# Half of the key page products of a paged decode moved from VectorE to GpSimd, in a hybrid decoder layer

## The chip, the core and the metric

One core of one Trainium2 chip runs the whole kernel in one launch. The metric is the device time of that core in microseconds. Engines are TensorE (PE), VectorE (DVE), ScalarE (ACT), GpSimd (POOL) and SyncE (SP); POOL and SP also issue the kernel's DMAs.

## What is computed

One inference step of one decoder layer, for a prompt of 256 tokens and for 8 samples of one token each (264 columns together). Width 2048; a combined input projection feeds two groups of heads: 8 heads of stick-breaking attention (head size 128) and 4 heads of gated linear attention; then an output projection and a SwiGLU FFN. The samples attend to a paged cache: 8 samples x 8 pages = 64 key pages and 64 value pages, each 128 positions x 8 heads x 128. The part that the change touches is the score of the samples against the cached keys:

```python
k_past = cache_k[l][page_table].reshape(dec_b, -1, SB_HEADS, SB_HEAD_DIM)
...
k_all = jnp.concatenate([k_past.astype(h.dtype), k_rows], axis=1).transpose(0, 2, 1, 3)
...
z = jnp.einsum('bhqd,bhkd->bhqk', q.astype(jnp.float32), k.astype(jnp.float32)) * (SB_HEAD_DIM ** -0.5)
...
a = jnp.where(mask, jnp.exp(log_beta + tail), 0.0)
return jnp.einsum('bhqk,bhkd->bhqd', a, v.astype(jnp.float32))
```

For one page and one sample this is, for each of 128 positions (partitions) and each head, the sum over 128 elements of key times query.

## The kernel before, in words

**Weight units and slots.** The input projection and the output projection are cut into 128 units of two 128-row blocks by 512 columns (groups of 8 units). Each unit goes through a ring of four buffers: SP loads it (`w_load`, L398), ACT makes a rounded high part (`hi`, L723, L727), DVE the low part (`lo`, L1275, L1277), and PE multiplies high and low parts with high and low parts of the activations, three products each (`products`, L1996 to L1999; `unit`, L2001). The program of each engine is a loop over slots, `st` in `range(NSLOT)`: in slot `st` PE multiplies unit `st`, ACT and DVE begin with the parts of unit `st + 3`, and behind that every engine does what is written by hand for this slot. ACT's high part waits until PE has used the unit four earlier, SP's load until the low part of the unit four earlier is made. Conditioning weights come as `ada_r` tiles of 1 MB in SP's queue (`ada_load`, L401), and PE uses one of them at the end of many slots (L1931).

**The decode path.** `KP_SLOT` says in which slot key page `n` is worked on: three pages in two slots from slot 20 to 31, one page a slot from 32 to 49, three in two slots from 50 to 68. PE spreads the query of a sample over all partitions (`query_rows`, L2025), ACT copies it to `QBC` (`q_bcast`, L802, L808; two buffers). Then:
- DVE, in slot `KP_SLOT[n]` behind its low part: `page_product` (L1316). An even page takes eight multiplications of 128x128 that also sum the head (L1328, semaphore `k_even`). An odd page takes one multiplication of 128x1024 in place (L1322, semaphore `k_mul`).
- ACT, in the slot after, near its end: `page_sums` (L810, L815) waits for `k_mul` and sums the eight heads of an odd page (semaphore `k_odd`). At the end of every eighth slot the evacuations of a group (`evac`, L729) stand behind it.
- POOL: `k_page` (L564 to L577) reads the page number from the table, waits until the page five earlier is done (`k_even` or `k_odd`, L572), and requests the page; five pages are in flight or in work. The request for page `n` stands in slot `KP_SLOT[n - 5] + (n - 5) % 2`: so a request that needs an odd page's sums stands in the slot in which ACT makes them, a request that needs an even page in the slot in which DVE multiplies it.

**Behind it.** In slots 47 and 70 DVE takes the scores of four samples each, in slots 53 and 76 ACT makes the weights, and PE multiplies them with value pages, two a slot (`page_values`, L2115, L2129), in slots 56, 57 and from 60 on (`AV_SLOT`). POOL requests value pages (`v_page`, L579, L595) in the same slots, each after PE has used the page five earlier. POOL also stores the states (`state_store`, L603) and rows of keys.

**The tree of the linear attention.** In slots 31 to 50, beside the key pages: DVE takes differences (`tree_diff`, L1335) in odd slots, ACT their exponential (`tree_exp`, L818) and DVE the products (`tree_product`, L1355) in even slots, PE multiplies (`tree_mm`, L2041, L2055) in odd slots, from slot 33 on.

The order of POOL's queue in one slot is: key page requests, value page requests, state store, stores of key rows:

```python
for n in range(5, TS * PAGES):
    if s == KP_SLOT[n - 5] + (n - 5) % 2:
        k_page(n)
...
if s in AV_AT:
    for m in (2 * AV_AT[s] + 5, 2 * AV_AT[s] + 6):
        if m < TS * PAGES:
            v_page(m)
if s in DEC_AT and DEC_AT[s] % 3 == 2:
    state_store(DEC_AT[s] // 3)
```

Of the kernel before, what the change touches and what calls it, by code (L numbers as in the profile page):

```python
# [10 lines left out]
ALU = mybir.AluOpType  # L11
# [7 lines left out]
def stickbreak_gla_layer(nc, x_prompt, x_sample, c_prompt, c_sample, cache_k, cache_v, page_table, state_gla,  # L19
# [10 lines left out]
    H = b_sb.shape[1]  # L30
    DH = g_sb_out.shape[1]
# [3 lines left out]
    PAGES = page_table.shape[1]  # L35
# [17 lines left out]
    with ctx:  # L53
        def sem(name):
            return ctx.enter_context(nc.semaphore(name))

        def sems(name, n):
            return [sem(f"{name}{i}") for i in range(n)]
# [7 lines left out]
        def put(name, shape, dt=F32, at=None):  # L66
            size = 4
            for s in shape[1:]:
                size *= s
            size = -(-size // 32) * 32  # L70
            if at is None:
                at = cursor[0]
                cursor[0] += size
            assert at + size <= top, (name, at + size, top)
            return nc.alloc_sbuf_tensor_at(name, shape, dt, offset=at)
# [81 lines left out]
        KPG = [put(f"k_page{i}", [P, HS], at=a) for i, a in enumerate(  # L157
            (r0 + 38016, r0 + 42112, r0 + 46208, r0 + 50304, r0 + 62592, r0 + 21120, r0 + 92544))]
# [7 lines left out]
        QBC = put("q_bcast", [P, 2, HS], at=r0 + 66688)  # L166
# [8 lines left out]
        ZD = put("z_dec", [P, TS, PAGES * H], at=r0 + 74880)  # L175
# [105 lines left out]
        KP_AT = {s: [n for n in range(TS * PAGES) if KP_SLOT[n] == s] for s in KP_SLOT}  # L281
        KP_PLACE = [n % 5 if n % 5 < 4 else 4 if n < 34 else 5 if n < 54 else 6 for n in range(TS * PAGES)]
# [34 lines left out]
        kpage_in = sems("kpage_in", 5)  # L317
# [17 lines left out]
        srow_ready, qlo_ready, qb_mm, qb_ready = sem("srow_ready"), sem("qlo_ready"), sem("qb_mm"), sem("qb_ready")  # L335
        k_mul, k_even, k_odd = sem("k_mul"), sem("k_even"), sem("k_odd")
# [190 lines left out]
        def _(pool):  # L527
            link = linker(pool, pool_own)
            g = nc.gpsimd
# [34 lines left out]
            def k_page(n):  # L564
                page = pool.value_load(PT[0:1, n:n + 1], min_val=0, max_val=NPOOL - 1)
                if n == 2:
                    pool.wait_ge(ada_used, 14)
                if n == 34:

                    pool.wait_ge(alp_ready, 1)  # L570
                if n >= 5:
                    pool.wait_ge(k_odd if (n - 5) % 2 else k_even, (n - 5) // 2 + 1)  # L572
                if n == 54:

                    pool.wait_ge(g_o, GH)
                pool.dma_start(KPG[KP_PLACE[n]][:, :], pool_k[bass.ds(page, 1), :, :].rearrange("o p n -> p (o n)"))\
                    .then_inc(kpage_in[n % 5], 16)  # L577

            def v_page(m):  # L579
                if m in (0, 1):  # L580
                    pool.wait_ge(kft_tr, 1)
                elif m == 2:
                    pool.wait_ge(g_st, 1)
                elif m == 3:
                    pool.wait_ge(vg_tr, 4)
                    pool.wait_ge(vsmp_ready, 1)
                elif m == 4:
                    pool.wait_ge(g_o, GH)
                else:
                    pool.wait_ge(av_used, (m - 5) // 2 + 1)  # L590
                if m == 32:
                    pool.wait_ge(k_even, 32)
                    pool.wait_ge(k_odd, 32)
                page = pool.value_load(PT[0:1, m:m + 1], min_val=0, max_val=NPOOL - 1)
                pool.dma_start((VPA if m < 32 else VPB)[m % 5][:, :],  # L595
                               pool_v[bass.ds(page, 1), :, :].rearrange("o p n -> p (o n)")).then_inc(vpage_in[m % 5], 16)

            def zero_rows():

                pool.wait_ge(ada_used, 32)  # L600
                g.memset(VGS[:, :].bitcast(F32), 0.0).then_inc(pool_made, 1)

            def state_store(c):  # L603
                h, half = divmod(c, 2)
                pool.wait_ge(dec_taken, 3 * c + 2)
                pool.dma_start(new_state_sample[0, 4 * half:4 * half + 4, h].rearrange("b k v -> k b v"),
                               SS[:, c % 3, :, :]).then_inc(state_out[c % 3], 16)
# [5 lines left out]
            for s in range(20, 97):  # L613
                if s == 58:

                    v_page(4)
# [3 lines that stand above are left out]
                if s in (53, 55):  # L620
                    v_page(s - 53)
                    v_page(s - 52)
                if s == 56:
                    pool.wait_ge(gla_copied, 2)
                    pool.dma_start(new_state_prompt[0, 0].rearrange("h k v -> k h v"), SFIN[:, :, :]).then_inc(sfin_out, 16)
                if s == 58:
                    zero_rows()
# [3 lines that stand above are left out]
                            v_page(m)  # L631
                if s in DEC_AT and DEC_AT[s] % 3 == 2:
                    state_store(DEC_AT[s] // 3)
                if s - 2 in KT_AT:
                    i = KT_AT[s - 2]
                    grp, tb = divmod(i, 2)
                    pool.wait_ge(kt_ready, i + 1)
                    pool.dma_start(kv_rows[tb * P:(tb + 1) * P, grp * 512:grp * 512 + 512], KTOK[i % 2][:, :])\
                        .then_inc(ktok_out[i % 2], 16)
# [24 lines left out]
            for m in range(MT - 1):  # L664
                pool.wait_ge(gm_ready, NOUT + 2 * m + 1)
                ins = g.tensor_tensor(SQD[:, 8, :], SQD[:, 8, :], SQD[:, X_LAST[m], :], ALU.add)
# [523 lines left out]
        def _(dve):  # L1190
            link = linker(dve, dve_own)
            v = nc.vector
# [123 lines left out]
            def page_product(n):  # L1316
                b = n // PAGES
                kp = KPG[KP_PLACE[n]]
                dve.wait_ge(kpage_in[n % 5], 16 * (n // 5 + 1))
                dve.wait_ge(qb_ready, 2 * b + 2)  # L1320
                if n % 2:
                    v.tensor_tensor(kp[:, :], kp[:, :], QBC[:, b % 2, :], ALU.mult).then_inc(k_mul, 1)  # L1322
                else:

                    pg = n % PAGES
                    for h in range(H):
                        hs = slice(h * DH, (h + 1) * DH)
                        ins = v.scalar_tensor_tensor(kp[:, hs], kp[:, hs], 1.0, QBC[:, b % 2, hs], ALU.mult, ALU.mult,  # L1328
                                                     accum_out=ZD[:, b, pg * H + h:pg * H + h + 1])
                    ins.then_inc(k_even, 1)  # L1330

            def halves(t, n):
                return t.rearrange("p h (j n) -> p h j n", n=n)
# [172 lines left out]
            def slot(st):  # L1506
# [38 lines left out]
                if st == 61:  # L1545
                    dve.wait_ge(srow_ready, 3)
                    for j in range(2):
                        cs = slice(j * 512, j * 512 + 512)
                        ins = v.tensor_tensor(VGS[32:32 + TS, cs], ps[0:TS, 5 + j, :], VGS[0:TS, cs].bitcast(F32),
                                              ALU.subtract)  # L1550
                    ins.then_inc(qlo_ready, 1)
                if st == 17:
                    dve.wait_ge(srow_ready, 1)
                    for half in range(2):
                        cs = slice(half * 512, half * 512 + 512)
                        ins = v.tensor_tensor(QHL[32:32 + TS, cs], ps[0:TS, 6 + half, :], QHL[0:TS, cs].bitcast(F32),
                                              ALU.subtract)
                    ins.then_inc(qlo_ready, 1)
                for n in KP_AT.get(st, ()):
                    page_product(n)  # L1560
                if st == 25:
                    dve.wait_ge(bank_out, 12)
                    v.tensor_scalar(PGQ[:, 0:GH, :], PGQ[:, 0:GH, :], GLA_SCALE, None, ALU.mult).then_inc(alp_ready, 1)
# [37 lines left out]
                if st == 87:  # L1601
                    dve.wait_ge(row_tr, 4)
                    for vb in range(VD):
                        ins = v.tensor_copy(PGQ[:, vb::VD, TP:T].rearrange("p h (f j) -> p h f j", f=2),
                                            ps[:, 4, vb * P:(vb + 1) * P].rearrange("p (j c) -> p j c", j=4)[:, :, 0:2 * GH]
                                            .rearrange("p j (h f) -> p h f j", f=2))
# [9 lines left out]
                if st == 89:  # L1616
                    dve.wait_ge(silu_r, 8)
                    dve.wait_ge(norm_sq, 1)
                    for vb in range(VD):
                        cs = slice(vb, 8, VD)  # L1620
                        ins = v.scalar_tensor_tensor(PGQ[:, cs, :], PGQ[:, cs, :], vec2[:, V2["gla"] + vb:V2["gla"] + vb + 1],
                                                     PR[:, cs, :], ALU.mult, ALU.mult)
# [98 lines left out]
            for st in range(NSLOT):  # L1721
                slot(st)
# [130 lines left out]
            for j in range(1, 5):  # L1853
                for u in range(4):
                    lo_n(j * 4 + W_DOWN, u)
                    k = 4 * j - 4 + u
                    ins = v.transpose(XT[:, :, k, :], X[:, k, 0:TP].rearrange("p (b j) -> p b j", j=32))  # L1857
# [33 lines left out]
            for m in range(8):  # L1891
                dve.wait_ge(tail_sq, m + 1)
                ins = v.tensor_tensor(F_LO[:, 0, :], F_LO[:, 0, :], F_LO[:, 8 + m, :], ALU.add)
# [674 lines left out]
```

## Time and profile before

| What | Value |
|---|---|
| Median of 3 runs | 1488.83 us (1487.38 to 1489.83) |
| Profiled execution, its own time | 1489.45 us |
| Its span, first to last instruction | 1487.7 us |
| Busy PE / DVE / ACT / POOL | 1428.6 / 922.3 / 665.3 / 105.8 us |
| Mean granted clock of PE | 0.983 of full speed |
| Moved by DMA | 396.82 MB, mean 267 GB/s |

The time lies 1.75 us above the span; what is worked out on the span is taken to move the time by as much. PE is busy for 96% of the span, but matmuls are pipelined and their ends are modelled, so busy PE is not PE at its peak; what matters is where it is idle. Busy shares are averages over stages: slots 20 to 68, in which key pages are worked on, take about 188 to 420 us of the span; the FFN takes the second half.

### The profile page before, as it was taken

Reading aid. Unit: us, or ns where it says so; the run is one execution under the profiler, and the core shown is the slowest. Engines: PE = TensorE matmul, PEld = TensorE weight load, DVE = VectorE, ACT = ScalarE, POOL = GpSimd, SP = SyncE. Lnnn points to the kernel's source line nnn. Section 1 sums busy time; section 2 is a strip of 40 time slices with the busy share of each in tenths; the row PEclk is TensorE's granted clock in tenths of the full one; section 3 lists DMA queues with packets and bytes.
Section 4 is the critical chain, followed back from the end, with each engine's and each line's share of the span. In section 5 each row is a group of like instructions: output and inputs, shape, how many; then the busy total and the mean of one; then the engine's idle time right before and its main releaser. Section 6 shows DMA issues by size and latency. Waiting matters only on the chain.

```text
span 1487.7 us, 29187 instructions
## 1 busy us (share of the span) xinstructions
PE 1428.6 (96%) x11232; PEld 1270.8 (85%) x11232; DVE 922.3 (62%) x1519; ACT 665.3 (45%) x1303; POOL 105.8 (7%) x203
## 2 busy tenths in 40 slices
PE   7779999999899999999999999999999999999997
PEld 2237787887668787796999999999999999999997
DVE  2234588996778667369856766566665675446444
ACT  1023477677655554445543434334344343334333
POOL 0000311113322210000000000000000000200000
PEclk9969999999899999999999999999999999999999
DMA  9999999999999979987666666665666655855552
GB/s 368 421 341 359 388 392 406 379 345 397 392 396 336 342 258 354 404 323 278 221 181 184 178 179 179 181 185 171 183 181 174 185 173 190 233 179 181 182 177 95
DMA packets 139330, 396.82 MB, mean 267 GB/s; under 512 B 13162, under 2 KB 17681, under 8 KB 126433
## 3 DMA queue, kind: packets, MB, share of 16 engines
q1 hardware_dynamic: 117954, 319.59, 63.1%
q0 software_dynamic: 21232, 76.10, 13.5%
q8 instruction: 49, 0.80, 0.2%
q14 instruction: 31, 0.25, 0.0%
q10 hardware_dynamic: 64, 0.07, 0.0%
HBM read 382.28 MB, written 11.34 MB: 265 GB/s over the span
## 4 chain that ended last, share of the span: by engine, by line
PE 84%; DMA 9%; DVE 3%; ACT 2%; issue 1%; POOLq 0%; SPq 0%; POOL 0%; DVEq 0%; ACTq 0%
PE ps L1997 24%; PE ps L1998 24%; PE ps L1999 24%; PE ps L1931 4%; DMA ada_s<-in_w_ada 4%; DMA v_page<-in_cache_v 2%; PE ps L2129 2%; DMA ada_r<-in_w_ada 1%; DMA k_page<-in_cache_k 1%; PE ps L2055 1%; ACT k_page L815 1%; PE ps L1974 0%; DVE k_page L1328 0%; DVE w_lo L1277 0%; ACT w_hi L727 0%
## 5 line engine op out<-in xcount | busy, mean ns | idle before, releaser
L1997 PE MATMUL ps<-h_hi,w_hi 128*128 128x264 f32 x2304 | 666.9, 289 | 6.1 <-DVE h_lo L1265 3.6
L1998 PE MATMUL ps<-h_lo,w_hi 128*128 128x264 f32 x2304 | 658.6, 286 | 0.0
L1999 PE MATMUL ps<-h_hi,w_lo 128*128 128x264 f32 x2304 | 658.2, 286 | 0.0
L1997 PEld LDWEIGHTS ps<-h_hi,w_hi 128*128 128x128 f32 x2304 | 438.1, 190 | 49.1 <-issue 33.6
L1822 DVE TENSOR_TENSOR w_lo<-raw,w_hi 128x1024 fp32r<-128x1024 f32 x254 | 307.2, 1214 | 273.1 <-ACT w_hi L1059 271.7
L1059 ACT ACTIVATE w_hi<-raw 128x1024 fp32r<-128x1024 f32 x264 | 278.5, 1059 | 403.2 <-PE ps L1999 391.0
L1998 PEld LDWEIGHTS ps<-h_lo,w_hi 128*128 128x128 f32 x2304 | 437.4, 190 | 0.5
L1999 PEld LDWEIGHTS ps<-h_hi,w_lo 128*128 128x128 f32 x2304 | 436.3, 189 | 0.0
L1277 DVE TENSOR_TENSOR w_lo<-raw,w_hi 128x1024 fp32r<-128x1024 f32 x138 | 168.8, 1224 | 144.4 <-ACT w_hi L727 143.9
L727 ACT ACTIVATE w_hi<-raw 128x1024 fp32r<-128x1024 f32 x128 | 135.1, 1056 | 174.7 <-PE ps L1999 156.3
L1998 PE MATMUL ps<-act_lo,w_hi 128*128 (+1 forms) x704 | 200.5, 285 | 0.0
L1997 PE MATMUL ps<-act_hi,w_hi 128*128 (+1 forms) x704 | 200.2, 284 | 0.0
L1999 PE MATMUL ps<-act_hi,w_lo 128*128 (+1 forms) x704 | 199.7, 284 | 0.0
L1997 PEld LDWEIGHTS ps<-act_hi,w_hi 128*128 128x128 f32 x704 | 132.5, 188 | 0.3 <-issue 0.2
L1998 PEld LDWEIGHTS ps<-act_lo,w_hi 128*128 128x128 f32 x704 | 132.6, 188 | 0.0
L1999 PEld LDWEIGHTS ps<-act_hi,w_lo 128*128 128x128 f32 x704 | 132.5, 188 | 0.0
L1815 DVE RECIPROCAL glu<-glu 128x264 f32<-128x264 f32 x44 | 78.8, 1792 | 0.0
L815 ACT ACTIVATE k_page<-k_page 128x128 f32<-128x128 f32 x256 | 75.2, 297 | 7.0 <-DVE k_page L1322 6.8
L1931 PE MATMUL ps<-ada_r,c_t_keep 128*32 128x512 f32 x512 | 66.3, 603 | 4.2 <-DMA ada_r<-in_w_ada 4.2
L1328 DVE SCALAR_TENSOR_TENSOR k_page<-k_page,q_bcast 128x128 f32<-128x128 f32 x256 | 56.9, 289 | 11.5 <-DMA k_page<-in_cache_k 11.4
L1931 PE MATMUL ps<-ada_s,c_t_keep 128*32 128x512 f32 x256 | 45.9, 799 | 18.1 <-DMA ada_s<-in_w_ada 18.1
L675 POOL DMA_DIRECT2D x_moved_blocks<-x_blocks x16 | 8.6, 546 | 585.2 <-DVE x_blocks L1857 585.2
(363 smaller groups left out, 1217.6 us busy)
## 6 DMA issues: line engine op xcount, KB each, us to landing
ada_r<-in_w_ada SPq DMA_DIRECT2D x64, 1024.0 KB, 8.9
raw<-in_w_in SPq DMA_DIRECT2D x96, 512.0 KB, 8.4
raw<-in_w_ffn_gate SPq DMA_DIRECT2D x88, 512.0 KB, 3.7
raw<-in_w_ffn_up SPq DMA_DIRECT2D x88, 512.0 KB, 3.8
raw<-in_w_ffn_down SPq DMA_DIRECT2D x88, 512.0 KB, 4.3
ada_s<-in_w_ada SPq DMA_DIRECT2D x32, 1024.0 KB, 13.2
k_page<-in_cache_k POOLq DMA_DIRECT2D x64, 512.0 KB, 7.9
v_page<-in_cache_v POOLq DMA_DIRECT2D x38, 512.0 KB, 8.0
```

The costliest lines, as they stand in the source:

```text
L727: s.activation(HI[:, u % 4, :], RAW[:, u % 4, :], ACT.Copy).then_inc(hi_ready, 1)
L815: ins = s.activation(kp, kp, ACT.Copy, accum_out=ZD[:, b, pg * H + h:pg * H + h + 1])
L1059: s.activation(HI[:, u % 4, :], RAW[:, u % 4, :], ACT.Copy).then_inc(hi_ready, 1)
L1277: v.tensor_tensor(LO[:, u % 4, :], RAW[:, u % 4, :], HI[:, u % 4, :].bitcast(F32), ALU.subtract)\
L1328: ins = v.scalar_tensor_tensor(kp[:, hs], kp[:, hs], 1.0, QBC[:, b % 2, hs], ALU.mult, ALU.mult, accum_out=ZD[:, b, pg * H + h:pg * H + h ...
L1815: v.reciprocal(GLU[:, m, :], GLU[:, m, :]).then_inc(glu_step, 1)
L1822: v.tensor_tensor(LO[:, u % 4, :], RAW[:, u % 4, :], HI[:, u % 4, :].bitcast(F32), ALU.subtract)\
L1931: ins = mm(ps[32 * j:32 * j + 32, bank, :], CTK[:, k, :], ring[:, j * CG:(j + 1) * CG], start=(k == 0), stop=(k == KC - 1))
L1997: mm(out, w_hi, xh, start=first, stop=False)
L1998: mm(out, w_hi, xl, start=False, stop=False)
L1999: return mm(out, w_lo, xh, start=False, stop=last)
L2129: ins = mm(ps[32 * j:32 * j + 32, 7, :], AD[:, b % 4, 2 * pair + j // 2, :], page, start=(v % 16 == 0), stop=(v % 16 == 15))
```

## The change

The product of an odd key page is no longer made by DVE in slot `KP_SLOT[n]` but by POOL in the same slot, behind POOL's key page requests, value page requests and state store of that slot. POOL waits there for the landing of the page and for the spread query. DVE keeps the even pages. ACT's sums, the requests and all slots stay as they are.

```diff
+            def odd_product(n):
+                kp = KPG[KP_PLACE[n]]
+                pool.wait_ge(kpage_in[n % 5], 16 * (n // 5 + 1))
+                pool.wait_ge(qb_ready, 2 * (n // PAGES) + 2)
+                g.tensor_tensor(kp[:, :], kp[:, :], QBC[:, n // PAGES % 2, :], ALU.mult).then_inc(k_mul, 1)
+
             def v_page(m):
...
                 if s in DEC_AT and DEC_AT[s] % 3 == 2:
                     state_store(DEC_AT[s] // 3)
+                for n in KP_AT.get(s, ()):
+                    if n % 2:
+                        odd_product(n)
                 if s - 2 in KT_AT:
...
                 dve.wait_ge(qb_ready, 2 * b + 2)
-                if n % 2:
-                    v.tensor_tensor(kp[:, :], kp[:, :], QBC[:, b % 2, :], ALU.mult).then_inc(k_mul, 1)
-                else:
-
-                    pg = n % PAGES
-                    for h in range(H):
...
+                pg = n % PAGES
+                for h in range(H):
...
                 for n in KP_AT.get(st, ()):
-                    page_product(n)
+                    if n % 2 == 0:
+                        page_product(n)
```

## Rows read from the trace of the kernel before

**Rows 1.** Stretch: us; busy PE, PEld, DVE, ACT, POOL; PE clock, DMA share, GB/s

```profile
213.00:243.00 30.00, 26.54 (x212) 22.29 (x211) 27.06 (x100) 22.13 (x94) 5.65 (x11) 1.00 1.02 402
...
242.00:320.00 78.00, 78.00 (x638) 69.79 (x635) 73.20 (x209) 57.51 (x199) 8.59 (x17) 1.00 0.99 377
...
345.00:375.00 30.00, 26.88 (x190) 22.31 (x188) 16.08 (x58) 20.93 (x74) 9.07 (x16) 0.94 1.04 397
375.00:425.00 50.00, 43.55 (x314) 33.55 (x311) 38.08 (x134) 31.00 (x138) 14.73 (x27) 0.90 1.03 392
```

**Rows 2.** Shares of the chain that ended last, by line, from 340 to 425 us

```profile
by line: DMA v_page<-in_cache_v 28.7%; DMA k_page<-in_cache_k 12.5%; issue 10.3%; PE ps L1997 7.8%; PE ps L2129 7.8%; PE ps L1998 6.8%; PE ps L1999 6.7%; DVE k_page L1328 3.9%; ACT k_page L815 2.5%; DVE gate_exp L1441 2.1%; PE ps L2176 2.0%
```

**Rows 3.** POOL's waits over the span: us in total, times, longest us

```profile
POOL k_page L576 <- ACT k_page L815: 98.3, 20, 10.2
POOL v_page L595 <- issue: 62.3, 38, 5.0
```

**Rows 4.** Groups by line, 190 to 430 us: busy us, mean ns; idle before, releaser

```profile
L1277 DVE TENSOR_TENSOR w_lo<-raw,w_hi 128x1024 fp32r<-128x1024 f32 x51 | 62.4, 1223 | 29.0 <-ACT w_hi L727 28.9
L1328 DVE SCALAR_TENSOR_TENSOR k_page<-k_page,q_bcast 128x128 f32<-128x128 f32 x256 | 56.9, 289 | 11.5 <-DMA k_page<-in_cache_k 11.4
L1322 DVE TENSOR_TENSOR k_page<-k_page,q_bcast 128x1024 f32<-128x1024 f32 x32 | 39.1, 1222 | 0.1
...
L815 ACT ACTIVATE k_page<-k_page 128x128 f32<-128x128 f32 x256 | 75.2, 297 | 7.0 <-DVE k_page L1322 6.8
L727 ACT ACTIVATE w_hi<-raw 128x1024 fp32r<-128x1024 f32 x51 | 53.7, 1053 | 43.4 <-PE ps L1999 37.6 <-DMA raw<-in_w_in 5.7
```

**Rows 5.** POOL in order of time: start us, duration us, what, idle before it

```profile
192.78 0.53 POOL L576 DMA_DIRECT2D k_page<-in_cache_k  x1 [8.57 <-DVE k_page L1328]
196.40 0.53 POOL L576 DMA_DIRECT2D k_page<-in_cache_k  x1 [3.09 <-ACT k_page L815]
197.56 0.53 POOL L576 DMA_DIRECT2D k_page<-in_cache_k  x1 [0.63 <-issue]
```

**Rows 6.** DVE in order of time: the first odd product, a low part, the ninth

```profile
192.04 1.22 DVE L1322 TENSOR_TENSOR k_page<-k_page,q_bcast 128x1024 f32<-128x1024 f32 x1
193.32 1.23 DVE L1277 TENSOR_TENSOR w_lo<-raw,w_hi 128x1024 fp32r<-128x1024 f32 x1
...
233.25 1.22 DVE L1322 TENSOR_TENSOR k_page<-k_page,q_bcast 128x1024 f32<-128x1024 f32 x1
```

**Rows 7.** POOL and DVE side by side, in order of time, at two places

```profile
679.11 0.76 POOL L666 TENSOR_TENSOR squares<-squares 128x264 f32<-128x264 f32 x1 [69.22 <-DVE mix_out L1741]
680.64 1.92 POOL L666 TENSOR_TENSOR squares<-squares 128x264 f32<-128x264 f32 x2 [0.78 <-DVE mix_out L1741]
...
679.50 0.66 DVE L1731 TENSOR_TENSOR squares<-squares 128x264 f32<-128x264 f32 x1 [0.49 <-ACT squares L1075]
...
680.61 0.43 DVE L1745 TENSOR_TENSOR squares<-mix_out,x_old 128x264 f32<-128x264 f32 x1
...
164.29 0.29 POOL L551 TENSOR_SCALAR_AFFINE_SELECT tree_mask<-ones 128x128 f32<-128x128 f32 x1
...
165.41 1.14 POOL L551 TENSOR_SCALAR_AFFINE_SELECT tree_mask<-ones 128x128 f32<-128x128 f32 x1
...
165.15 1.26 DVE L1277 TENSOR_TENSOR w_lo<-raw,w_hi 128x1024 fp32r<-128x1024 f32 x1
```

**Rows 8.** POOL's widest instruction that is no request, from the groups by line

```profile
L601 POOL MEMSET vgs_rows<- 72x1024 f32 x1 | 1.0, 980 | 0.0
```

**Rows 9.** PE in order of time: tree products of slots 33 and 35

```profile
242.49 1.95 PE L2055 MATMUL ps<-tree 128*128 128x128 f32 x16
...
251.57 0.60 PE L2055 MATMUL ps<-tree 128*128 128x128 f32 x4
```

**Rows 10.** POOL in order of time: requests of key page 41 and value page 21

```profile
322.56 0.53 POOL L576 DMA_DIRECT2D k_page<-in_cache_k  x1 [1.29 <-DVE k_page L1328]
...
412.48 0.53 POOL L595 DMA_DIRECT2D v_page<-in_cache_v  x1 [4.17 <-issue]
```

More of the change, by code:

```diff
@@ L1320, in page_product @@
                 dve.wait_ge(qb_ready, 2 * b + 2)
-                if n % 2:
-                    v.tensor_tensor(kp[:, :], kp[:, :], QBC[:, b % 2, :], ALU.mult).then_inc(k_mul, 1)
-                else:
-                    pg = n % PAGES
-                    for h in range(H):
[L1327 to L1330, printed above, removed]
+                pg = n % PAGES
+                for h in range(H):
+                    hs = slice(h * DH, (h + 1) * DH)
+                    ins = v.scalar_tensor_tensor(kp[:, hs], kp[:, hs], 1.0, QBC[:, b % 2, hs], ALU.mult, ALU.mult,
+                                                 accum_out=ZD[:, b, pg * H + h:pg * H + h + 1])
+                ins.then_inc(k_even, 1)
             def halves(t, n):
```

## Prediction

> **What bounds the kernel now.** I read the stretches first, then the chain, then the waits, and last single instructions. The change touches slots 20 to 68. By the windows [rows 1] TensorE is never idle from 242 to 320 us, and loses 3.5 us of 30 (213 to 243), 3.1 of 30 (345 to 375) and 6.5 of 50 (375 to 425): 13 us in all. That is the most that relief of DVE alone could bring. DVE is busy for 73.2 of 78 us in the middle stretch, and the DMA share is 0.99 to 1.04 throughout: three resources lie close together. Where TensorE does lose time, the chain from 340 to 425 us goes through landings of value pages (28.7%) and key pages (12.5%), that is, through requests on GpSimd's queue [rows 2]. GpSimd is idle most of the time, but its waits say what paces it: 98.3 us for ACT's sums of odd pages, 62.3 us (the row calls it issue) ahead of value pages [rows 3]. It is a queue that must be free at the right moment, not a free engine.
>
> **The prices.** In that stretch [rows 4] an odd product costs DVE 39.1/32 = 1.22 us, the eight multiplications of an even page 56.9/32 = 1.78 us, ACT's eight sums 75.2/32 = 2.35 us, a low part 1.22 us, a high part 1.05 us. ACT lost only 6.8 us to DVE's odd products. A GpSimd request behind another starts 1.16 us after it (197.56 less 196.40), and takes 0.53 us [rows 5]. One released by a sum starts 0.75 us after it: product 1 ends on DVE at 193.3 [rows 6], 2.35 us of sums later it is 195.65, and the request starts at 196.40.
>
> GpSimd's product of 128x1024 does not occur. Nearest row: its sum of 128x264, 0.76 us alone [rows 7]. Two behind one another take 1.92 us, the first of them waiting for DVE's 680.61 to 681.04; what is left gives about 0.60 us of reading for 264 elements and 0.16 fixed. 0.60 x 1024/264 + 0.16 = 2.5 us, which I take, because it is the same operation. Upper end: all of the 0.76 scales, 2.95 us. Lower end: no dearer than the memset of the same width, 0.98 us [rows 8]. The Trainium skill (GPSIMD Engine Reference, Elementwise — side-by-side cycle accounting) gives 4497 ns for an add of 2048 fp32; half of it, an estimate, is 2.25 us, and would take 5 us off the sum below.
>
> Do the two engines get in each other's way? An affine select that takes 0.29 us takes 1.14 us when it starts 0.26 us behind a low part on DVE, and ends 0.15 us behind that (166.41). The other way, DVE's sum of 128x264, 0.43 us elsewhere, takes 0.66 us under GpSimd's [rows 7]. So one excludes the other, and I count 0.5 us (0 to 1.2, the length of a low part) ahead of each product, and up to 2.35 us in which DVE stands still. The rule is in the Trainium skill (SBUF — State Buffer, Who interferes with whom): a DVE instruction with two SBUF inputs and a GpSimd instruction that reads SBUF block each other whole. By it, DVE gives away 1.22 us and may lose 2.35; without it, it gains 1.22.
>
> **What moves, and the new loop.** DVE loses 32 x 1.22 = 39 us of work, and its wait for odd pages. GpSimd gets 32 products. Before, products never waited for GpSimd beyond the landing. Now the queue closes on itself: product of an odd page (GpSimd), its sums (ACT, next slot), the request that waits for these sums at the head of GpSimd's next slot, further requests, next product. All is in program order on one queue, so nothing overlaps. ACT waits in order too: behind its sums stand the next high part, hence the low part, hence TensorE. One round costs 2.35 sums + 0.75 release + 0.53 request + 0.1 + 0.5 + 2.5 product = 6.8 us (with the second 0.1 of ACT's start), and 1.16 us for each further request. Three places:
>
> Slots 20 to 31. Three pages in two slots. The request of page 5 is at 192.78 [rows 5]; product 1 starts at 193.4, meets the low part that began at 193.32 [rows 6] until 194.5, and ends at 196.9. Products 3 to 17 are 8 rounds: 54.4 us. Between them stand 16 requests, 8 of them inside the rounds; the other 8 cost 9.3 us. Three times (slots 22, 26, 30) the request wants an even page whose low part comes behind ACT's late high part: 1.05 + 1.22 + 1.78 + 0.7 against some 3.1 us of requests, 1.5 us each, 4.5 us. Product 15 ends at 196.9 + 7 x 6.8 + 9.3 + 4.5 = 258.3, its sums at 260.7; behind them come four evacuations of 264 columns, a high part and the first tree exponential on ACT and the tree product on DVE, each about 1024 columns wide; by the high and the low part's prices an estimate of 3 x 1.05 + 1.22 = 4.4 us, and about 1 us of exclusion. That brings TensorE's first tree product to 266, where it stood at 242.49. By product 17 (265.1) and its sums the second stands at about 273 instead of 251.57 [rows 9]: +22 us. TensorE's lead of three weight units doesn't help, since it wants the tree and the spread query of the slot itself. DVE's 1.22 us saved are free there, because it then waits.
>
> Slots 32 to 49. One odd page in two slots (9.1 us from tree product to tree product [rows 9]): the round of 6.8 + 1.16 fits, and the product falls ahead of ACT's need. Here the exclusion counts: DVE has 73.2/78 x 9 = 8.4 us of work, less 1.22, plus up to 2.35 = 9.6 against TensorE's 9. Nine pairs make 0 to 6 us; I take 2, as part of a product falls on DVE's idle time or on work from PSUM.
>
> Slots 50 to 68. Request 41 starts at 322.56, that of value page 21 at 412.48 [rows 10]: 89.9 us. Between them the queue now has 46 requests x 1.16 = 53.4, a memset 1.0, 12 products x 3.1 = 37.2 (with start and exclusion), 11 waits for sums x 2.6 = 28.6, and two even pages 3.0: 123.2 us, +33. Value pages are the critical landings here already, so there is no cover; ACT's lateness goes the same way. Afterwards the pace is as before (two value pages per slot), and the rest is bound by TensorE, so nothing is given back.
>
> **Sum.** +22 + 2 + 33 = +57 on the profiled execution (1489.45 us around a span of 1487.7; the median of the runs is 1488.83, 0.6 lower): 1546 us on the median. Ends: 21 products on the two chains. At 0.98 us they take 32 off, and no loss in the middle 2, so 1512; at 2.95 us, with 1.2 us of exclusion, they add 24, and the middle 4, so 1574.
>
> **Rivals.**
> 1. The excluded port alone: rounds hide behind ACT's other work and TensorE's lead, and only DVE's standing still counts. Price: 2.35 less 1.22, so 1.13 us net x 32 = 36 us on DVE, of which its idle time (3 of 30, 5 of 78, 12 of 50 us in [rows 1]) hides some two thirds: about +12, 1501. For it: DVE's 94% in the middle. Against: ACT waits in order, and GpSimd's requests stood after the sums already. The rule named above is what decides here.
> 2. Half cover: one of the two dense places is hidden, say because ACT's sums start before the next high part is wanted. +24 to +35, 1513 to 1524.
> 3. The other side: DVE gets 39 us free, even pages and low parts come earlier, and requests with them. It decides if GpSimd's product ends before ACT's slot wants it, so if a round is below the 5.2 us from one of DVE's odd products to the next in slots 20 to 31 (192.04 to 233.25, 8 steps [rows 6]). It then gives at most the idle time blamed on late low parts and key pages, some 6 of the 13 us: 1483. Against: ACT's sums and one request alone are 3.6 us, so the product would have 1.6 us, wait and all.
> 4. No change: the DMA share near 1.0 sets the end, both kernels move the same bytes, 1489. Against: from 460 us on TensorE is the bound, and what the queue asks late can't land early.
>
> **How the numbers follow.** Differences under 0.2% (3 us) can't be told from none. Forecast 0.70, rival 1 0.09, rival 2 0.14, rival 3 0.04, rival 4 0.03. The likeliest case gives 1546. The range takes in the forecast's own ends and rival 2: 1510 to 1575; outside lie rivals 1, 3 and 4 and what the ends miss. Faster 0.04, same 0.03, slower 0.93.
>
> **What would show it.** Right: GpSimd's product has a median near 2.5 to 3 us in the groups by line; ACT's idle time before its sums grows from 7 to over 60 us, released by GpSimd; the request's wait for ACT is made of pieces of some 2.5 us, once per product; tree products start near 266 and 273; DVE's low part shows some of 2 to 3.5 us; TensorE's idle time and low granted clock grow between 205 and 270 and beyond 340, and from some 510 us on all is as before, shifted. Wrong: ACT waits below 15 us in all (rival 1 or 3); a product below 1.5 us; the shift all in the middle stretch (rival 1).

## The result, and the profile after

The changed kernel takes **1554.15 us** (median of 5 runs, 1553.65 to 1555.65), the kernel before 1489.83 in the same session (5 runs, 1487.38 to 1492.74): ratio 1.0433, 95% interval 1.042 to 1.0446, so 64.3 us slower. Forecast were 1546 and 1510 to 1575. The profiled execution took 1553.92 us around a span of 1552.3 (before: 1487.7).

The windows of the kernel after, with the columns of [rows 1]:

```profile
213.00:243.00 30.00, 24.91 (x184) 21.61 (x184) 21.41 (x79) 14.94 (x68) 14.04 (x12) 0.94 0.86 301
...
345.00:375.00 30.00, 21.57 (x171) 18.30 (x169) 22.96 (x84) 14.90 (x67) 12.93 (x12) 0.96 0.89 307
375.00:425.00 50.00, 38.74 (x243) 30.80 (x244) 26.98 (x90) 29.05 (x110) 23.53 (x27) 0.85 0.86 308
425.00:460.00 35.00, 23.24 (x162) 17.96 (x161) 17.17 (x58) 13.02 (x61) 16.27 (x19) 0.80 0.82 295
460.00:500.00 40.00, 30.00 (x186) 21.44 (x185) 27.58 (x61) 20.66 (x85) 15.78 (x18) 0.79 0.87 299
500.00:540.00 40.00, 40.00 (x322) 32.07 (x321) 31.36 (x61) 24.70 (x54) 7.95 (x14) 1.00 0.94 331
```

TensorE lost 3.5 of 30 us in the first of these before [rows 1] and loses 5.1 now; from 375 to 500 us it is idle for 33 of 125. DVE, ACT and the DMA share have fallen with it: every engine waits, GpSimd included (busy for 23.5 of 50 us at most). From 500 to 540 us TensorE is again never idle.

The shares by line of the chain that ended last, 370 to 485 us, the same work as in [rows 2]:

```profile
by line: issue 21.5%; POOL k_page L583 20.7%; ACT k_page L824 19.9%; POOLq L600 5.2%; POOL v_page L601 4.9%; PE ps L2135 4.8%; PE ps L2003 3.0%; PE ps L2004 2.4%; PE ps L2005 2.3%; POOLq L565 2.2%; POOL k_page L576 1.9%; ACT w_hi L736 1.7%;
```

The landings of pages (28.7% and 12.5% before) are no longer among the lines shown ("issue", 21.5%, is time for which the profile shows no wait). In their place stand the product on GpSimd (L583) and ACT's sums of it (L824), one behind the other: that is the loop.

The waits of the kernel after, 190 to 500 us (in total, times, longest, us):

```profile
POOL k_page L576 <- ACT k_page L824: 109.6, 29, 7.0
ACT k_page L824 <- POOL k_page L583: 96.4, 24, 6.4
DVE w_lo L1286 <- ACT w_hi L736: 79.6, 27, 8.7
...
POOL v_page L601 <- issue: 34.4, 28, 7.8
...
PE ps L2003 <- ACT proj_t L744: 20.2, 3, 9.2
...
PE ps L2045 <- ACT q_bcast L817: 12.4, 2, 7.3
```

GpSimd waits for ACT and ACT for GpSimd, each some 100 us in all. The wait for value pages, 62.3 us over the whole span before [rows 3], is 50.2 over the whole span now (34.4 of it in this stretch): GpSimd comes to them late. The first row alone would have shown little (98.3 before, 109.6 now). What tells is that the same wait is now answered by one in the other direction, 7.0 us before [rows 4], 96.4 now.

Groups by line of the kernel after, 190 to 500 us, as [rows 4]:

```profile
L1333 DVE SCALAR_TENSOR_TENSOR k_page<-k_page,q_bcast 128x128 f32<-128x128 f32 x256 | 81.8, 381 | 0.0
L583 POOL TENSOR_TENSOR k_page<-k_page,q_bcast 128x1024 f32<-128x1024 f32 x32 | 80.3, 2508 | 0.5
L824 ACT ACTIVATE k_page<-k_page 128x128 f32<-128x128 f32 x256 | 75.4, 296 | 96.4 <-POOL k_page L583 96.4
L1286 DVE TENSOR_TENSOR w_lo<-raw,w_hi 128x1024 fp32r<-128x1024 f32 x51 | 71.5, 1403 | 79.6 <-ACT w_hi L736 79.6
...
L1349 DVE TENSOR_TENSOR tree<-cum 128x512 f32<-128x512 f32 x7 | 20.7, 2954 | 0.0
```

And the last of them in the kernel before, 190 to 500 us:

```profile
L1344 DVE TENSOR_TENSOR tree<-cum 128x512 f32<-128x512 f32 x7 | 4.8, 689 | 0.0
```

The product takes 2.51 us, wait and all. DVE stands still under it: an even page's multiplication has a mean of 381 ns instead of 289, the low part 1403 instead of 1223 [rows 4], and the tree difference, 689 ns before, 2954. Added up, 81.8 less 56.9, 71.5 less 51 x 1.22 and 20.7 less 4.8 are 24.9 + 9.1 + 15.9 = 50 us, more than the 39 us of products that DVE was relieved of.

One round of the loop, GpSimd in order of time (columns of [rows 5]):

```profile
202.33 0.53 POOL L576 DMA_DIRECT2D k_page<-in_cache_k  x1 [2.22 <-DVE k_page L1333]
202.87 2.35 POOL L583 TENSOR_TENSOR k_page<-k_page,q_bcast 128x1024 f32<-128x1024 f32 x1
208.35 0.59 POOL L576 DMA_DIRECT2D k_page<-in_cache_k  x1 [3.13 <-ACT k_page L824]
208.96 2.39 POOL L583 TENSOR_TENSOR k_page<-k_page,q_bcast 128x1024 f32<-128x1024 f32 x1
214.49 0.59 POOL L576 DMA_DIRECT2D k_page<-in_cache_k  x1 [3.14 <-ACT k_page L824]
215.65 0.53 POOL L576 DMA_DIRECT2D k_page<-in_cache_k  x1 [0.57 <-issue]
216.20 2.39 POOL L583 TENSOR_TENSOR k_page<-k_page,q_bcast 128x1024 f32<-128x1024 f32 x1
```

A product ends at 205.22, ACT's sums take 2.35 us, the request starts 3.13 us after the product's end and the next product 0.61 after that. That is 6.09 us from product to product (2.35 + 3.13 + 0.61), and 7.24 with a second request. The third kind of step, with a wait for an even page, takes 10.0 (192.88 to 202.87). The three follow one another from slot 20 to 31, 23.3 us for three products.

The tree products that answer to [rows 9] (of the first, the view's window ends before the last 3 of 16 matmuls), and the requests that answer to [rows 10]:

```profile
264.55 1.61 PE L2061 MATMUL ps<-tree 128*128 128x128 f32 x13
...
273.62 0.60 PE L2061 MATMUL ps<-tree 128*128 128x128 f32 x4
```

```profile
352.37 0.53 POOL L576 DMA_DIRECT2D k_page<-in_cache_k  x1 [2.71 <-DVE k_page L1333]
...
468.70 0.59 POOL L601 DMA_DIRECT2D v_page<-in_cache_v  x1 [1.06 <-issue]
```

With these the delay can be cut into the forecast's places. The second tree product is 22.1 us late (273.62 less 251.57), and request 41 29.8 (352.37 less 322.56), so the middle gave 7.7. Value page 21 is 56.2 late, so 26.4 fell between. The last 8.4 come until slot 70: ACT's high part of that slot is 65 us late, and from slot 74 or so on the distance stays at 64.7, close to the 64.6 by which the spans differ.

### The profile page after: what moved, and what is told of

It reads as the page before. It is cut to its first block, busy times and chain, and to the rows that moved or that the text cites. A ratio compares the mean times of both kernels' runs of the same rounds, so it can differ in the third digit from the quotient of the medians.

```text
span 1552.3 us, 29187 instructions
## 1 busy us (share of the span) xinstructions
PE 1449.5 (93%) x11232; PEld 1281.9 (83%) x11232; DVE 944.0 (61%) x1487; ACT 663.6 (43%) x1303; POOL 187.9 (12%) x235
## 4 chain that ended last, share of the span: by engine, by line
PE 73%; DVE 6%; DMA 5%; ACT 5%; POOL 4%; issue 4%; POOLq 1%; SPq 0%; DVEq 0%; ACTq 0%
PE ps L2003 21%; PE ps L2004 21%; PE ps L2005 21%; PE ps L1937 4%; ACT k_page L824 3%; POOL k_page L583 3%; DMA ada_s<-in_w_ada 3%; DVE k_page L1333 2%; PE ps L2135 2%; DVE w_lo L1286 1%; DMA sxx_keep<-x_sq_sum 1%; DMA ada_r<-in_w_ada 1%; ACT w_hi L736 1%; DVE tree L1349 1%; PE ps L1980 1%
## 5 line engine op out<-in xcount | busy, mean ns | idle before, releaser
L2003 PE MATMUL ps<-h_hi,w_hi 128*128 128x264 f32 x2304 | 669.7, 291 | 24.9 <-ACT proj_t L744 20.2
L1828 DVE TENSOR_TENSOR w_lo<-raw,w_hi 128x1024 fp32r<-128x1024 f32 x254 | 307.1, 1213 | 273.1 <-ACT w_hi L1068 271.8
L1286 DVE TENSOR_TENSOR w_lo<-raw,w_hi 128x1024 fp32r<-128x1024 f32 x138 | 177.8, 1290 | 197.5 <-ACT w_hi L736 197.0
L824 ACT ACTIVATE k_page<-k_page 128x128 f32<-128x128 f32 x256 | 75.4, 296 | 96.4 <-POOL k_page L583 96.4
L1333 DVE SCALAR_TENSOR_TENSOR k_page<-k_page,q_bcast 128x128 f32<-128x128 f32 x256 | 81.8, 381 | 0.0
L583 POOL TENSOR_TENSOR k_page<-k_page,q_bcast 128x1024 f32<-128x1024 f32 x32 | 80.3, 2508 | 0.5
## 6 DMA issues: line engine op xcount, KB each, us to landing
ada_s<-in_w_ada SPq DMA_DIRECT2D x32, 1024.0 KB, 12.7
```

Source lines behind the costliest of these rows:

```text
L583: g.tensor_tensor(kp[:, :], kp[:, :], QBC[:, n // PAGES % 2, :], ALU.mult).then_inc(k_mul, 1)
L824: ins = s.activation(kp, kp, ACT.Copy, accum_out=ZD[:, b, pg * H + h:pg * H + h + 1])
L1286: v.tensor_tensor(LO[:, u % 4, :], RAW[:, u % 4, :], HI[:, u % 4, :].bitcast(F32), ALU.subtract)\
L1828: v.tensor_tensor(LO[:, u % 4, :], RAW[:, u % 4, :], HI[:, u % 4, :].bitcast(F32), ALU.subtract)\
L2003: mm(out, w_hi, xh, start=first, stop=False)
```

## The experiments

The theory is the forecast's: a product on the queue that issues the requests closes a loop with ACT's sums, and its whole length counts in the dense places. The rivals are that DVE's exclusion alone costs the time, and that the occupied queue alone does, with the requests issued later. What stands in brackets behind a time is its ratio to the kernel before and the 95% interval of the ratio; a number with a plus sign is the difference of the medians in us. The kernels of one part ran on one chip with their own runs of the kernel before.

### Where: one stretch of pages at a time

Three kernels give GpSimd only pages 1 to 17, 19 to 35 or 37 to 63, and DVE the other odd ones. The fourth, p_ahead, gives it all 32, but ahead of the slot's requests.

```diff
+        def by_pool(n):
+            return n % 2 == 1 and 0 <= n < 18
...
-                    if n % 2:
+                    if by_pool(n):
                         odd_product(n)
...
+                if n % 2:
+                    v.tensor_tensor(kp[:, :], kp[:, :], QBC[:, b % 2, :], ALU.mult).then_inc(k_mul, 1)
+                    return
...
-                    if n % 2 == 0:
+                    if not by_pool(n):
                         page_product(n)
```

(This is p_early; 18 to 36 in p_mid, 36 to 64 in p_late; ACT's sums wait for whichever engine made the product.) And p_ahead:

```diff
+                for n in KP_AT.get(s, ()):
+                    if n % 2:
+                        odd_product(n)
                 for n in range(5, TS * PAGES):
                     if s == KP_SLOT[n - 5] + (n - 5) % 2:
                         k_page(n)
...
-                for n in KP_AT.get(s, ()):
-                    if n % 2:
-                        odd_product(n)
```

> Of the 32 odd products only the 9 of slots 20 to 31 (pages 1 to 17) are made by GpSimd, the others by DVE as in the kernel before. Theory A, the closed loop (product, sums, request, product in order on GpSimd's queue): the second tree product (before 251.57 us, after 273.62) stands near 273.6 again, and the whole time rises by that shift, +20 to +24 us, since TensorE gives nothing back later. Theory B, the excluded port alone (a product costs what DVE stands still, so the cost goes by the number of products): 9/32 of the measured +64, +18 us, with ACT's idle time before its sums small. The two differ in where the time lies: A wants ACT to wait some 30 us for GpSimd here, B under 5.

> Only the 9 odd products of slots 33 to 49 (pages 19 to 35) are made by GpSimd. Theory A: the round of 8 us fits into the 9 us between two odd pages, so only DVE's standing still counts, +2 to +8 us (the trace after shows +8 between the second tree product and request 41). Theory B: 9/32 of +64, +18 us.

> Only the 14 odd products of slots 50 to 68 (pages 37 to 63) are made by GpSimd. Theory A: the queue's own work binds: +33 to +37 us (predicted +33 up to value page 21; in the trace after the stretch behind request 41 grows by 35). Theory B: 14/32 of +64, +28 us, spread evenly over the products.

> All 32 odd products on GpSimd, but each in front of its slot's requests instead of behind them: nothing is computed otherwise. The product of page n then no longer waits for the sums of the odd page before it. Theory A: the round falls apart; ACT makes the sums beside GpSimd's next product, ACT's idle time before its sums falls from 96 us to under 30, and what stays is DVE's standing still and GpSimd's own work in slots 60 to 68: +8 to +25 us against before, 1498 to 1515. Theory B: the same products and the same exclusion, so about +60, 1550.

Measured against 1491.57 us: p_early 1510.79 (1.013, 1.0113 to 1.0146), +19.2; p_mid 1497.89 (1.0047, 1.003 to 1.0064), +6.3; p_late 1523.42 (1.022, 1.0203 to 1.0237), +31.9; together 57.4. p_ahead 1506.73 (1.0109, 1.0092 to 1.0126), +15.2. ACT's waits for GpSimd between 190 and 560 us in p_early, p_late and p_ahead, one fence for each:

```profile
ACT k_page L829 <- POOL k_page L588: 30.1, 9, 5.6
```

```profile
ACT k_page L829 <- POOL k_page L588: 60.1, 13, 6.5
```

```profile
ACT k_page L824 <- POOL k_page L583: 28.4, 16, 4.2
```

The early and the late pages carry their terms of the sum, 22 and 33, if a little less than was expected of each alone (19.2 for 20 to 24, 31.9 for 33 to 37). In p_early the second tree product is 20.9 us late and the way from request 41 to value page 21 takes 89.6 us, as before (89.9): the late part makes its own delay and is not an echo of the early one. p_ahead answers the main question. It has all 32 products on GpSimd, as long (2508 ns) and excluding DVE as much, as its groups by line show (31 of the 32 lie between 190 and 560 us):

```profile
L1333 DVE SCALAR_TENSOR_TENSOR k_page<-k_page,q_bcast 128x128 f32<-128x128 f32 x252 | 90.0, 418 | 3.3 <-DMA k_page<-in_cache_k 3.3
L583 POOL TENSOR_TENSOR k_page<-k_page,q_bcast 128x1024 f32<-128x1024 f32 x31 | 77.7, 2508 | 2.1 <-DMA k_page<-in_cache_k 1.7
...
L1349 DVE TENSOR_TENSOR tree<-cum 128x512 f32<-128x512 f32 x7 | 21.1, 3016 | 0.0
```

DVE's multiplications and differences are if anything slower than after the change, and yet it costs a quarter as much. So 49 of the 64 us hang on where the product stands in the queue: behind the request that waits for the last sums, it can't start before they are done; ahead of it, it runs while ACT makes them. How the 15.2 us that stay divide between the occupied queue, the exclusion and DVE's relief isn't shown.

### What: the queue, the port and the loop taken apart

Here DVE makes all products, as before the change. GpSimd gets, where the changed kernel has its product, work of about the same length (here called a mark) on space that nothing else uses: eight memsets of 128x256 (d_write, which read nothing), or three products of 128x256 (d_read). GpSimd waits for the end of a mark before it goes on. The edits are shown against the kernel before. In d_gate ACT's sums also wait for the eight memsets, so the loop is closed without a read of SBUF; d_gate2 has sixteen.

```diff
+            def mark(n, s):
+                d = DUM[0 if s < 60 else 1]
+                pool.wait_ge(kpage_in[n % 5], 16 * (n // 5 + 1))
+                pool.wait_ge(qb_ready, 2 * (n // PAGES) + 2)
+                for j in range(8):
+                    ins = g.memset(d[:, :], 0.0)
+                    if j < 7:
+                        link(ins)
+                ins.then_inc(k_mark, 1)
+                pool.wait_ge(k_mark, 32 + n // 2 + 1)
...
                 if s in DEC_AT and DEC_AT[s] % 3 == 2:
                     state_store(DEC_AT[s] // 3)
+                for n in KP_AT.get(s, ()):
+                    if n % 2:
+                        mark(n, s)
```

In d_read the loop holds `g.tensor_tensor(d[:, :], d[:, :], d[:, :], ALU.mult)` three times, and the space is cleared once before; d_gate and d_gate2 add one line to `page_sums`:

```diff
                 act.wait_ge(k_mul, n // 2 + 1)
+                act.wait_ge(k_mark, 32 + n // 2 + 1)
```

> The kernel before (DVE makes all products), but GpSimd does, at the places where the change puts its product and behind the same waits, 8 memsets of 128x256 on unused space, some 2.5 us that write and don't read; nobody waits for them. It tells what the occupied queue costs by itself: requests late by up to 2.5 us, no exclusion on the read side, no closed loop. Theory A: +3 to +15 us, most of it from slot 50 on, where value pages are the critical landings. Theory B (exclusion alone): 0 to +2 us.

> As the kernel with the memsets, but with 3 products of 128x256 each on unused space instead (some 2.3 us that read SBUF); nobody waits for them and DVE makes all key page products. The difference to the kernel with the memsets is the price of the exclusion. Theory A: +10 to +25 us against before, so 7 to 15 us more than with the memsets, and DVE's low parts and tree differences longer. Theory B: all of the +64 and more, since DVE has its own 39 us on top.

> As the kernel with the memsets, but ACT's sums wait for the memsets as well as for DVE's product: the closed loop without exclusion. Theory A: the loop alone brings back most of the loss, +40 to +55 us (64 less some 8 for the exclusion in the middle, less what the exclusion adds to each round), and the stretch from request 41 to that of value page 21 is near 116 us again. Theory B: as with the memsets alone, under +5 us.

> As the kernel whose sums wait for the memsets, but 16 memsets instead of 8: the occupation of the queue doubled, some 5 us. Theory A: every round on the two dense stretches gets longer by the full 2.5 us, 9 + 14 rounds, +55 us on the kernel with 8, and in the middle a round of 10.5 us no longer fits into 9.1 us, 9 x 1.4 = +13: about +65 in all, near 1600 us. A rival in which ACT's other work covers part of a round expects well under +40.

Measured against 1490.08 us: d_write 1504.63 (1.009, 1.0073 to 1.0107), +14.6; d_read 1525.16 (1.0232, 1.0215 to 1.0249), +35.1; d_gate 1562.05 (1.0482, 1.0465 to 1.05), +72.0; d_gate2 1643.72 (1.1034, 1.1016 to 1.1053), +153.6.

Groups by line of d_write, 190 to 560 us:

```profile
L586 POOL MEMSET dummy<- 128x256 f32 x256 | 81.1, 317 | 12.9
...
L1338 DVE TENSOR_TENSOR k_page<-k_page,q_bcast 128x1024 f32<-128x1024 f32 x32 | 39.1, 1222 | 0.4 <-DMA k_page<-in_cache_k 0.4
```

The same of d_read:

```profile
L586 POOL TENSOR_TENSOR dummy<-dummy 128x256 f32<-128x256 f32 x96 | 94.4, 983 | 5.5
...
L1341 DVE TENSOR_TENSOR k_page<-k_page,q_bcast 128x1024 f32<-128x1024 f32 x32 | 48.0, 1500 | 0.0
L1363 DVE TENSOR_TENSOR tree<-cum 128x512 f32<-128x512 f32 x7 | 7.7, 1097 | 0.0
```

Memsets leave DVE's products at 1222 ns, products of GpSimd bring them to 1500: the exclusion needs a read by GpSimd. That is what the Trainium skill says (SBUF — State Buffer, SBUF: two separate sides: a DVE instruction with two SBUF inputs is blocked only by a GpSimd one that reads SBUF), and these traces agree. Between d_write and d_read lie 20.5 us, the price of 32 reading stretches of 2.95 us each; an occupied queue alone costs 14.6. d_read missed what was expected of it (+10 to +25, and 7 to 15 above d_write): the exclusion is dearer than I had taken it. Of its 20.5 us, 6.2 lie before the second tree product, 9.7 between it and request 41, and the rest behind.

The wait of ACT's sums for the memsets, and one memset group in order of time, in d_gate:

```profile
ACT k_page L832 <- POOL dummy L586: 110.8, 23, 8.4
...
210.81 2.92 POOL L586 MEMSET dummy<- 128x256 f32 x8
```

and in d_gate2:

```profile
ACT k_page L832 <- POOL dummy L586: 183.6, 30, 10.9
...
216.39 5.89 POOL L586 MEMSET dummy<- 128x256 f32 x16
```

Closing the loop turns 14.6 us into 72.0, with no read, no exclusion and DVE's work unchanged. That shows the mechanism by itself. In size both missed what was expected: +72.0 for +40 to +55, and d_gate2 lies 81.7 us above d_gate where some 65 were expected. In d_gate the second tree product is 29.4 us late (22.1 after the change), and the way from request 41 to value page 21 takes 126.1 us, where "near 116" was expected. Part of the reason is plain: eight memsets take 2.92 us where I had reckoned with 2.5, some 0.4 us more in each round. d_gate2 measures how the time goes with the length. 2.97 us more a mark cost 81.7 us. Of these 16.8 fell between the second tree product (306.25) and request 41 (71.5 us late, the tree product 54.7), where d_gate's lost nothing; the other 64.9 make 21.9 us for each us of mark. Divided by place, 25.3 us came before the second tree product and 39.6 behind request 41, so 8.5 and 13.3 for each us of mark, where the forecast had counted 9 and 12 products, 21 on the two dense chains. By the same slope d_gate with marks of 2.5 us would cost about 63 us instead of 72, an estimate. That is about what the change costs, though DVE keeps its 39 us of products here and GpSimd excludes nothing; how these two weigh against each other isn't told apart.

### Can it be kept? The middle alone, the dense places alone

m_ahead has the middle pages by GpSimd, ahead of the requests; x_ahead has the 23 pages of the dense places so, and the middle ones on DVE. Both have p_ahead's placing with `by_pool` in the place of `n % 2`, and DVE and ACT's sums as in p_early; the edit of m_ahead, against the changed kernel:

```diff
+        def by_pool(n):
+            return n % 2 == 1 and 18 <= n < 36
...
+                for n in KP_AT.get(s, ()):
+                    if by_pool(n):
+                        odd_product(n)
                 for n in range(5, TS * PAGES):
                     if s == KP_SLOT[n - 5] + (n - 5) % 2:
...
-                for n in KP_AT.get(s, ()):
-                    if n % 2:
-                        odd_product(n)
```

(x_ahead: `n % 2 == 1 and not 18 <= n < 36`.)

> Only the 9 odd products of slots 33 to 49 on GpSimd, in front of the slot's requests instead of behind them. Theory A: in the middle the round never bound, and the loss (+6 us behind the requests) is DVE standing still under GpSimd's product, which the order doesn't touch: +4 to +10 us again, with the first half of the tree difference above 2 us on average as before. A rival, in which the middle too loses by the order (sums, requests, product): 0 to +2 us.

> The 23 odd products of slots 20 to 31 and 50 to 68 on GpSimd in front of the requests, the 9 in the middle on DVE. Theory A: +15 us with all 32 in front, less the +6 of the middle: +6 to +12 us, still slower than the kernel before, because GpSimd's queue is late for value pages by its products. A version that beats the kernel before would have to show under 0; the rival that the two dense places cost nothing once the loop is broken expects -3 to +3.

Against 1490.08 us (11 runs, 1488.13 to 1492.86): m_ahead 1497.82 (1.0051, 1.0039 to 1.0063), +7.7; x_ahead 1500.63 (1.0069, 1.0056 to 1.0082), +10.6. The middle costs as much ahead of the requests as behind them (+7.7 and +6.3), so it isn't the loop there. The tree differences of m_ahead:

```profile
L1357 DVE TENSOR_TENSOR tree<-cum 128x512 f32<-128x512 f32 x7 | 18.6, 2656 | 0.0
```

as in p_mid (2663 ns each), while p_late has them at 680 and no delay in the middle. With memsets in their place (d_write, d_gate) the middle loses nothing either (request 41 as late as the second tree product, 6.2 and 29.4 us); with products on idle space (d_read) it loses 9.7. So the middle's price is the exclusion: it is there with every kind of reading work on GpSimd and gone without it.

No version beats the kernel before. The best with all products on GpSimd is p_ahead, 1.1% slower.

## Why the prediction was right, and where not

**The loop.** Right, as mechanism and in its sign. ACT waits 96.4 us for products where "over 60" was forecast; d_gate makes the delay from the loop alone, p_ahead takes most of it away by order alone, and no rival does either. 21 products on the chains were forecast; with memsets in their place, d_gate2 less d_gate gives 21.9. One sign was off: the request's wait for ACT came in pieces of 3.13 us, where some 2.5 were forecast.

**The round.** 6.8 us forecast, 6.09 measured. The product's price of 2.5 came out as 2.35 to 2.39 us, a request and a sum as written. (Its working doesn't show in [rows 7], where two sums are merged: the first of them alone takes 1.00 us from 680.64 to 681.64, 0.60 behind the end of DVE's at 681.04.) The main error is the 0.5 us of exclusion ahead of each product: the mean of 2508 ns leaves 0.13 us over the usual 2.38, and nearly all of it lies in the middle, where the nine products have a mean of 2.80 us. In the dense places DVE mostly waits for the high part when the product starts, and it is DVE that runs into the product, not the other way round. The steps beside the rounds were right: 9.3 + 4.5 = 13.8 us forecast, 62.7 (192.88 to 255.61) less 8 x 6.09 = 14.0 measured.

**Slots 20 to 31, +22.** 22.1 measured (19.2 with these pages alone), but that it fits so well is luck: two errors nearly cancel. Product 15 ended at 251.86, not at 258.3: 6.4 us earlier. From there to the tree product it took 12.7 us, not 7.7. What was left out is TensorE itself. I wrote of its lead of three units, but the evacuations behind the sums hold it up as well, as three rows of the kernel after show (its windows, with the columns of [rows 1], and its first product after the wait):

```profile
248.00:250.00 2.00, 0.00 (x0) 0.00 (x0) 2.00 (x6) 0.00 (x0) 1.01 (x2) 0.94 0.90 323
...
258.00:260.00 2.00, 2.00 (x11) 2.00 (x11) 2.00 (x10) 1.97 (x14) 0.00 (x0) 0.50 0.36 139
260.00:262.00 2.00, 2.00 (x18) 2.00 (x18) 2.00 (x11) 1.43 (x5) 0.59 (x1) 1.00 0.78 214
```

```profile
254.76 0.56 PE L2003 MATMUL ps<-h_hi,w_hi 128*128 128x264 f32 x1 [9.25 <-ACT proj_t L744]
```

It stood still for 9.25 us, then had two units, 48 matmuls, to do before the tree product, and the first 24 of them ran at a granted clock of 0.50, its 1.2 GHz level, 0.22 us apart instead of 0.12: some 2.4 us more.

**Slots 32 to 49, +2.** Too small: 7.7 in the trace, 6.3 by itself. The value was for products that fall partly on DVE's idle time. They hardly do, and this is the step that failed; even the upper end (0 to 6) was too low. ACT's high part right behind its sums, GpSimd and DVE of the kernel after, at one of the places:

```profile
311.23 1.05 ACT L736 ACTIVATE w_hi<-raw 128x1024 fp32r<-128x1024 f32 x1
```

```profile
311.98 0.59 POOL L576 DMA_DIRECT2D k_page<-in_cache_k  x1 [5.71 <-ACT k_page L824]
313.13 0.53 POOL L576 DMA_DIRECT2D k_page<-in_cache_k  x1 [0.57 <-issue]
313.68 2.38 POOL L583 TENSOR_TENSOR k_page<-k_page,q_bcast 128x1024 f32<-128x1024 f32 x1
```

```profile
312.62 1.21 DVE L1286 TENSOR_TENSOR w_lo<-raw,w_hi 128x1024 fp32r<-128x1024 f32 x1
313.75 2.86 DVE L1349 TENSOR_TENSOR tree<-cum 128x512 f32<-128x512 f32 x1
```

The end of ACT's sums, behind which the high part starts at 311.23, starts both: GpSimd's two requests and product (2.45 us later), and ACT's high part, DVE's low part and tree difference (2.52 us later). One event and two ways of the same length, so they meet each time: all seven tree differences start within 0.6 us of a product, and one that took 0.69 us now ends only some 0.5 us after the product (here at 316.61, the product at 316.06). The seven, six of them in this stretch, cost (20.7 less 4.8) 15.9 us of DVE. All in all DVE was busy for 75.3 of 80.1 us from the first tree product (242.5) to request 41 (322.6) before the change, and is for 84.1 of 87.9 us now (264.5 to 352.4), although 9 x 1.22 = 11.0 us were taken off it: it lost some 20 us to nine products, 2.2 us each and not a part of 2.35. That is the upper case of the prediction's own term, for which it had 6 us; 7.7 came, as DVE still has 3.8 us of idle time between its pieces of work. TensorE, never idle there before, is idle for 6.3 us. An average over the stretch can't show that; the two queues laid side by side from their common release could have.

**Slots 50 to 68, +33.** 34.8 in the trace, 31.9 by itself, but spread otherwise. Between request 41 and value page 21 it took 116.3 us against 123.2 forecast. The 12 products there take 28.9 us, where 37.2 were reckoned with start and exclusion: 8.3 less; the other terms together took 1.4 more. The step that ended too soon is the sum's end at value page 21: products 61 and 63 and their sums are still to come, and 8.4 us with them. "From some 510 us on all is as before, shifted" held; the shift is all but complete at slot 70, whose high part starts at 490 us. How those 8.4 us divide between the two products, evacuations and states isn't settled.

**The rivals.** The port alone (1501, decided by the rule named there) was refuted as an explanation by d_gate and p_ahead, though its own price is real: 20.5 us between d_write and d_read, and the whole of the middle. Half cover fell with p_early and p_late. No change at all fell with the time: the DMA share, near 1.0 before, lies at 0.82 to 0.89 between 345 and 500 us now. That DVE's relief would bring anything was never seen; p_ahead, the kindest placing of all 32, is still 15.2 us slower. Open is why the three parts alone give 57.4 us and the whole 64.3.

## What to carry to other kernels

Before moving work to an engine that also issues requests, write out that engine's queue and look for a circle: if the moved instruction stands behind a request that waits for its own predecessor's result, nothing of its length is hidden where the rounds leave no slack, whatever the engine's busy share (in the middle, with some 9 us for a round, it was hidden). Place it ahead of the request, then ask what the other engine pays. For that, follow both queues from the event that releases them; if their ways are of the same length, a collision is the rule and not a chance.

## What the runs showed of the hardware

- Eight memsets of 128x256 fp32 on GpSimd take 2.92 us, 317 ns each beside DVE's work with no delay to it; products of the same size take 983 ns each, waits for DVE included. The memset of [rows 8] (72x1024, 980 ns) was a poor lower bound for a product of 128x1024, 2.35 to 2.39 us.
- The exclusion is lopsided here by circumstance: 0.13 us on average ahead of a GpSimd product, 2.3 us for each of the seven tree differences on DVE. Once, between 190 and 500 us, the product itself took 4.17 us.
- TensorE, idle from 245.51 us, is granted 0.94 of its clock from 248 to 250 us and 0.50 beyond, and is still at 0.50 for the first 5 us of its work. From 375 to 500 us, where it is often idle, the granted clock averages 0.79 to 0.85. What share of the delay that makes was not measured.
